# Fused encoder layer with product-key experts: the look-ahead shrinks from 96 to 72 expert blocks, and VectorE's and GpSimd's work around it is laid out anew

## What is computed

```
q  = rms_norm(h @ w_query)                    # 8 heads x 256
s1, s2 = scores of each half against 128 keys # top 16 of each
top_score, expert_idx = top 16 of the 256 sums # an index below 16384, per head
gate = softmax(top_score)
act  = gelu(u[expert_idx] . h) * gate          # 128 experts per token
x    = x + sum(act * v[expert_idx])
```

## Time and profile before

| | us |
|---|---|
| median of 3 runs (lowest, highest) | 3359.02 (3358.28, 3362.66) |
| the profiled execution: its own time | 3356.09 |
| its span, first to last instruction | 3354.4 |
| mean granted TensorE clock | 0.948 |
| TensorE busy | 2977.8 (89%) |
| VectorE busy | 2421.1 (72%) |
| GpSimd busy | 1695.2 (51%) |
| ScalarE busy | 1167.4 (35%) |
| DMA moved | 923.63 MB, 275 GB/s over the span |

### The profile page before, as it was taken

How to read it: one execution, slowest core, us unless ns; L and a number is a source line. 1 busy time by engine, 2 the same in 40 slices (tenths; PEclk the granted TensorE clock), 3 DMA queues, 4 the chain that set the end, 5 groups by cost and what they waited for, 6 DMA issues and landing times.

```text
span 3354.4 us, 43376 instructions
## 1 busy us (share of the span) xinstructions
PE 2977.8 (89%) x17829; PEld 2793.4 (83%) x17829; DVE 2421.1 (72%) x3297; ACT 1167.4 (35%) x1317; POOL 1695.2 (51%) x665
## 2 busy tenths in 40 slices
PE   6899899865989999987777998988888888999998
PEld 5677787644869999987777998888888888999998
DVE  5656566542676599997787345898888888767776
ACT  6756433344333333332222233222222222333332
POOL 0000443311232378864333687677677767667763
PEclk9999999977999999999888998999999999999999
DMA  7747458822696766656766998888888888888886
GB/s 299 266 163 286 156 215 311 311 75 86 261 359 259 264 242 235 235 181 206 244 213 212 339 381 335 329 339 328 327 335 327 317 336 335 325 345 335 345 326 233
DMA packets 196478, 923.63 MB, mean 275 GB/s; under 512 B 17712, under 2 KB 83360, under 8 KB 93376
## 3 DMA queue, kind: packets, MB, share of 16 engines
q1 hardware_dynamic: 85136, 479.24, 38.6%
q0 software_dynamic: 56112, 406.05, 32.0%
q10 hardware_dynamic: 55104, 36.71, 3.5%
HBM read 876.25 MB, written 45.61 MB: 275 GB/s over the span
## 4 chain that ended last, share of the span: by engine, by line
PE 47%; DVE 25%; DMA 15%; ACT 6%; issue 5%; ACTq 1%; POOL 1%; SPq 0%; DVEq 0%; POOLq 0%
PE ps L1473 6%; DMA rows<-peer_u_rows,idx_far 5%; PE ps L1782 5%; PE ps L1784 5%; PE ps L1783 5%; PE ps L1713 5%; PE ps L1714 5%; PE ps L1715 5%; DVE rows L1199 5%; PE ps L1698 3%; PE ps L1460 3%; DMA g_in<-gelu_scratch 3%; DVE g_in L1357 3%; DVE hot_b L1341 2%; DVE ring_lo L986 2%
## 5 line engine op out<-in xcount | busy, mean ns | idle before, releaser
L530 POOL TENSOR_TENSOR ring_lo<-ring_raw,ring_hi 128x2048 fp32r<-128x2048 f32 x252 | 1191.6, 4729 | 1047.0 <-ACT ring_hi L603 1045.8
L603 ACT ACTIVATE ring_hi<-ring_raw 128x2048 fp32r<-128x2048 f32 x400 | 763.6, 1916 | 696.8 <-DMA ring_raw<-w_in 204.6
L1782 PE MATMUL ps<-a_hi,ring_hi 128*128 128x320 f32 x2048 | 651.6, 318 | 102.9 <-DVE yT L1379 88.5
L1713 PE MATMUL ps<-bT_hi,ring_hi 128*128 128x320 f32 x2048 | 650.2, 317 | 10.1 <-ACT ahead L903 5.3
L1783 PE MATMUL ps<-a_lo,ring_hi 128*128 128x320 f32 x2048 | 643.8, 314 | 0.0
L1784 PE MATMUL ps<-a_hi,ring_lo 128*128 128x320 f32 x2048 | 643.4, 314 | 0.0
L1714 PE MATMUL ps<-bT_lo,ring_hi 128*128 128x320 f32 x2048 | 642.4, 314 | 0.0
L1715 PE MATMUL ps<-bT_hi,ring_lo 128*128 128x320 f32 x2048 | 641.8, 313 | 0.0
L986 DVE TENSOR_TENSOR ring_lo<-ring_raw,ring_hi 128x2048 fp32r<-128x2048 f32 x148 | 378.1, 2567 | 167.6 <-ACT ring_hi L603 167.3
L1782 PEld LDWEIGHTS ps<-a_hi,ring_hi 128*128 128x128 f32 x2048 | 394.6, 193 | 119.1 <-DVE yT L1379 96.6
L556 POOL DMA_INDIRECT rows<-peer_u_rows,idx_far x128 | 222.8, 1740 | 509.5 <-DVE z_far L1199 482.8
(11 more groups left out here) (285 smaller groups left out, 4171.7 us busy)
## 6 DMA issues: line engine op xcount, KB each, us to landing
ring_raw<-peer_u SPq DMA_DIRECT2D x128, 1024.0 KB, 5.3
ring_raw<-peer_v SPq DMA_DIRECT2D x128, 1024.0 KB, 7.3
ring_raw<-w_in SPq DMA_DIRECT2D x80, 1024.0 KB, 4.9
ring_raw<-w_out SPq DMA_DIRECT2D x32, 1024.0 KB, 5.0
ring_raw<-w_query SPq DMA_DIRECT2D x32, 1024.0 KB, 4.9
gates_scratch<-gbuf ACTq DMA_DIRECT2D x20, 1024.0 KB, 12.5
g_pair<-gates_scratch SPq DMA_DIRECT2D x64, 320.0 KB, 8.1
gelu_scratch<-ahead ACTq DMA_DIRECT2D x96, 160.0 KB, 5.5
```

The costliest lines, as they stand in the source:

```text
L530: pool.tensor_tensor(ring_lo[s][:], ring_raw[s][:], ring_hi[s][:].bitcast(F32), ALU.subtract)\
L603: act.activation(ring_hi[place(n)][:], ring_raw[place(n)][:], ACT.Copy).then_inc(hi_ok[SLOT[n]], 1)
L1713: pe.matmul(dst, hi[:, e], bT_hi[:, k, 0:NEAR], start=(k == 0), stop=False)
L1782: pe.matmul(dst, hi[:, col], a_hi[:, par, e, :], start=(e == 0), stop=False)
```

## The change

- `PRE` goes from 96 to 72: 24 blocks fewer in ahead and in down, 24 more in both (56 pairs). The downs are 68, the plain ups after the gate batches 5 instead of 29.
- In down (and for the first four blocks, during the last two ups) ScalarE copies `g_in` into a PSUM bank that is free (`gelu_to_psum`), and the gate product and the low half are made from PSUM. The product moves ahead of the row, the low half behind it.
- In the gate batches the low halves of four pieces in six, and of the last ahead pieces, go to VectorE; the other two stay on GpSimd. The one-hot ring gets a third place, `hot_b` is one instruction for four tokens, VectorE builds up to three sets ahead. The batch is 4, 4, 4, 4, 0, 0 outer products per up instead of 3, 3, 3, 3, 3, 1. The rows there go 1, 0, 1, 0, 2, 2.
- GpSimd issues a gather when the buffer's last row is 2 pieces behind, from the down stage on.
- The rows are spread anew: 60 instead of 47 at pieces 92 to 111 (20 instead of 12 of them in the attention), 28 and 30 instead of 28 and 28 at the two projections, 30 in the gate batches as before, 8 after them (38), 75 in down (123), 140 in both (77).
- In the attention ScalarE takes the two heads of a pair together through Abs, Exp and Ln; VectorE takes two rows ahead of the softplus and three behind the mask; the squares of y are summed in two parts.

```diff
-PRE = 96
+PRE = 72
 def lo_on_pool(n):
-    if n in POOL_A or AHEAD <= n < BOTH:
+    if n in POOL_A or DOWN <= n < BOTH or AHEAD <= n < AHEAD + HOT_FIRST:
         return True
+    if AHEAD <= n < DOWN:
+        return (n - AHEAD - HOT_FIRST) % len(HOT_BATCH) < 2
...
-ATTEND_ROWS = 12
+ATTEND_ROWS = 20
+HOT_RING = 3
+HOT_BATCH = (4, 4, 4, 4, 0, 0)
+HOT_ROWS = (1, 0, 1, 0, 2, 2)
...
+def gather_lag(n):
+    return 2 if n >= DOWN else ROW_LAG
...
-                gather_freed_before(n + 1 - ROW_LAG)
+                gather_freed_before(n + 1 - gather_lag(n))
...
             def load_gelu(i):
                 sp_eng.wait_ge(ahead_stored[i % 2], 16 * (i // 2 + 1))
                 if i >= 2:
-                    sp_eng.wait_ge(alo_made, i - 1)
+                    sp_eng.wait_ge(in_psum, i - 1)
...
+            def gelu_to_psum(i, bank):
+                act.wait_ge(gin_loaded[i % 2], 16 * (i // 2 + 1))
+                act.activation(ps[:, bank, 0:NEAR], g_in[i % 2][:], ACT.Copy).then_inc(in_psum, 1)
...
             for i in range(GROUP, PRE):
-                n = DOWN + i - GROUP
+                v = i - GROUP
+                n = DOWN + v
+                act.wait_ge(y_added, 4 * v + 1)
+                act.wait_ge(alo_made, GROUP)
+                gelu_to_psum(i, i % 4)
                 hi_upto(n + 2)
...
+            def hot(jj):
+                if jj >= HOT_RING:
+                    dve.wait_ge(g_mm, jj - HOT_RING + 1)
+                first, tok = 4 * (jj % HOT_RING), 4 * jj
+                for q in range(4):
+                    dve.tensor_scalar(hot_a[:, first + q, :], iota[:], selT[:, 0, tok + q:tok + q + 1],
+                                      selT[:, 2, tok + q:tok + q + 1], ALU.is_equal, ALU.mult)
+                dve.tensor_tensor(hot_b[:, first:first + 4, :], bcast(iota[:], [P, 4, NK], 1),
+                                  bcast(selT[:, 1, tok:tok + 4], [P, 4, NK], 2), ALU.is_equal).then_inc(hot_made, 1)
...
                 if v:
                     add_y(v - 1, 3)
-                rows_step(1 if ROWS_AT[n] else 0)
-                add_y(v, 0)
-                gate_down(i)
-                add_y(v, 1)
-                rows_step(ROWS_AT[n] - (1 if ROWS_AT[n] else 0))
+                dve.wait_ge(in_psum, i + 1)
+                gate(i, src, i // 4 + 1)
+                rows_step(1)
+                gated_lo(i, src)
+                add_y(v, 0)
+                add_y(v, 1)
+                rows_step(ROWS_AT[n] - 1)
                 add_y(v, 2)
...
-                    if k % 5 == 4 and k // 5 < gates_at:
+                    if k % 4 == 3 and k // 4 < gates_at:
                         outers()
...
-                    down(c, g + (USE0[c] + PRE // 4 + 1), 16 * g + 4 * c, c, par)
+                    down(c, g + (USE0[c] + PRE // 4 + 1), 16 * g + 4 * c, c, par, own=4 * g + (c + GROUP + 1))
```

More of the change, by code:

```diff
@@ L109, in fill_rows @@
             ROWS_AT[AHEAD + AHEAD_TILE * t + 2 + 2 * r] = 1
-    for i in range(HOT_FIRST, PRE):
-        ROWS_AT[AHEAD + i] = 1 if i < HOT_FIRST + 30 or i % 3 else 2
+    for i in range(HOT_FIRST, HOT_END):
+        ROWS_AT[AHEAD + i] = HOT_ROWS[(i - HOT_FIRST) % len(HOT_ROWS)]
+    for i in range(HOT_END, PRE):
+        ROWS_AT[AHEAD + i] = 2 if i < PRE - 2 else 1
     for n in range(DOWN, BOTH):
-        ROWS_AT[n] = 2 if n % 3 == 0 else 1
-    left = N_ROWS - sum(ROWS_AT)
-    spots = list(range(BOTH, LAST))
+        ROWS_AT[n] = 2 if n % 10 == 0 else 1
+    left, spots = N_ROWS - sum(ROWS_AT), range(BOTH, LAST)
     for j, n in enumerate(spots):
@@ L956, in _ @@
                 if i % GROUP == 0 and i > GROUP:
-                    act.wait_ge(freed[SLOT[n - 1]], USE[n - 1])
-                a_hi_of(i, g_in[i % 2][:])
+                    wait_piece(act, n - 1)
+                a_hi_of(i, ps[:, i % 4, 0:NEAR])
             for m in range(NK - PRE):
@@ L1253, in _ @@
                     norm_qk(i + 1)
+                rows_step(2)
                 for ab in range(2):
@@ L1361, in gate, with gate_first, hots_upto @@
                    .then_inc(alo_made, 1)
-            def gate_down(i):
-                dve.wait_ge(gin_loaded[i % 2], 16 * (i // 2 + 1))
-                gate(i, g_in[i % 2][:], i // 4 + 1)
+            def gate_first(i):
+                src = ps[:, i % 2, 0:NEAR]
+                dve.wait_ge(in_psum, i + 1)
[10 more added lines that the diff above has]
+                                  bcast(selT[:, 1, tok:tok + 4], [P, 4, NK], 2), ALU.is_equal).then_inc(hot_made, 1)
+            jj = [0]
+            def hots_upto(count):
+                while jj[0] < min(count, N_HOT):
+                    hot(jj[0])
+                    jj[0] += 1
+            hots_upto(HOT_RING)
+            used = 0
+            for i in range(HOT_FIRST, PRE):
+                lo_upto(min(AHEAD + i + 2, DOWN - 1))
+                used += HOT_AT[i]
+                hots_upto(used + HOT_RING)
+                if i < PRE - 2:
+                    rows_step(ROWS_AT[AHEAD + i])
+                else:
+                    gate_first(2 * (i - PRE + 2))
+                    rows_step(ROWS_AT[AHEAD + i])
+                    gate_first(2 * (i - PRE + 2) + 1)
+            assert jj[0] == N_HOT
             def v_piece(v):
@@ L1379, in add_y @@
                     dve.tensor_tensor(dst, src, dst, ALU.add).then_inc(y_added, 1)
-            for i in range(GROUP):
-                gate_down(i)
             for i in range(GROUP, PRE):
```

92 lines of the change are left out of this document (52 added, 40 removed).

## The result

The changed kernel takes **3227.89 us** (median of 4 runs, 3213.22 to 3231.14) against 3360.84 (3358.28 to 3370.47, 4 runs) of the kernel before beside it: ratio 0.9592, 95% interval 0.9562 to 0.9623, so 133 us faster by the medians. The forecast was 3152 with a range of 3095 to 3225: the sign and most of the mechanisms were right, the size too large. The median lies 3 us above the range; the ratio, put on the 3359.02 from which the forecast started, gives 3222, just inside it.

What follows compares the result with a forecast made beforehand. VectorE, stretched by GpSimd's low halves, slowed down, the largest term. Down -294, both +334, plain ups -177, change to down -4.5, batches -59, input +21, attention -27 gave -206.5 from 3356.09; with 2.9 for the median, 3152 us (3095 to 3225).

Steps and rivals of the forecast that it cites:

- Down, -294: Down: with product and low half made from PSUM, 68 pieces at 7.25 us, 493 us against 787.
- the chain of `g_in`: Down: from load issue to halved gate, 2T = L + 5.35 us; load time L = 8.7 gives 7.04 a piece.
- The sign that I had named for this being wrong: Down: VectorE's gate product waiting for `g_in` in most pieces would show the forecast wrong.
- the first rival: Down: the load of `g_in` sets the pace at 8.0 us or more, +51, 3203 us; chance 0.17.
- Only operations with both inputs in SBUF are stretched.: VectorE in down: the product from SBUF takes 1585 ns in the mean, from PSUM 496, beside a busy GpSimd.
- Both, +334: Both: 24 more pairs at 13.84 us, +332, and 2 us added.
- Ups, batches, change to down, -240.5: 24 fewer plain ups -177, change to down -4.5, gate batches at 68 us each -59.
- Before the expert layer, -6: Input stage +21 for its added rows; attention -27 from its new order of work.
- Transfers did not bound both: Rival: transfers bound both at 7.38 us a piece, and down too; +50 and +9, 3211 us; chance 0.11.
- the stores did hold the sixth up: Rival, gate batches: stores don't hold up the sixth up, batches of 58 us, -50 more, 3102 us; chance 0.12.
- the product from PSUM was not stretched: Rival: the product from PSUM is stretched all the same, down stays at 8.55 us, +88, 3240 us; chance 0.03.
- gathers sooner did no harm: Rival, down and both: gathers issued sooner delay GpSimd's low halves, making the kernel slower, 3368 us; chance 0.03.

Runs made afterwards that it cites:

- experiment 1: The changed kernel with gate product and low half reading the loaded gelu in SBUF again from the fifth block of down on; 3341.68 us, ratio 0.9942.
- experiment 2: The changed kernel with the loads of gates and gelu of down issued ahead of the piece load instead of behind it; 3202.23 us, ratio 0.9517.
- experiment 7: The changed kernel with all low halves of the gate batches on GpSimd again; 3249.93 us, ratio 0.9692.
- g1_combined: The changed kernel with earlier gelu loads, split stores, earlier row counts in input stage and attention, first gates ahead of the last ups' rows; 3135.40 us, ratio 0.9348.
- Experiment 9: The run of g1_combined: five edits put together on the changed kernel, among them both first gates ahead of the rows in the last two ups; 3135.40 us.
- Experiments 4: The changed kernel with the row counts ahead of the expert layer as in the kernel before; 3196.74 us, ratio 0.9495.
- experiment 10: g1_combined with 30 instead of 35 rows in the input stage and 8 instead of 12 in attention; 3125.75 us, ratio 0.9286.
- e5_pre96: The changed kernel with the split at 96 blocks again (PRE = 96), all the rest as changed; 3259.60 us, ratio 0.9696.
- e2_stores_split: The changed kernel with a batch's four gate stores split, two behind the fourth up's gelu and two behind the fifth's; 3199.73 us, ratio 0.9511.

## Why the prediction was right in sign and too large

**Down, -294 against -275.7.** The main step held: operations with one input in PSUM at 0.50 us, the clock at 0.99, VectorE no longer the bound (experiment 1). The term was mis-sized by the chain of `g_in`. I put L = 8.7 us and said that 10 would give 7.7 a piece; the stage came out at 7.53, although the loads landed in 4.7 / 7.5 / 10.6 us (shortest, median, longest), so that by my formula the median would have done no harm. Which link of that chain I had too short is open. The sign that I had named for this being wrong did show: VectorE's gate product waited for the copy of `g_in` in 44 of 68 pieces, 68.9 us in all. It was the first rival in kind, though not in size (+18 instead of +51), and experiment 2 shows it by taking the wait away.

One statement of the prediction is too narrow, without harm to the sum: "Only operations with both inputs in SBUF are stretched." `hot_a` takes one tile from SBUF, and it averaged 532 ns before where one undisturbed takes 340; experiment 7 shows it again.

**Both, +334 against +336.1.** Right to 2 us, but by luck, since two errors cancel. The price of a pair was 0.3 us too low (7 us for 24): 443 us divided by 32 pairs gave 13.84, while the window held 31.3 pairs, and from gelu to gelu a pair takes 14.14 before. And where I added 2 us for the denser traffic, a pair became 0.06 us shorter, 14.08 (774.5 over 55), 3 us in all. The transfers do not bound it: TensorE is busy for all of it, at a share of 0.90. At 0.93 (g1_combined) 13 rows more cost 10 us.

**Ups, batches, change to down, -240.5 against -233.8.** The batches came out as forecast. From one batch's stores to the next's pass 67.6 to 68.2 us, where I said 68: 24.3 from the stores to the gelu of the sixth up (24 said), with the gelu of the fourth held for 14.5 (16.8 said) and TensorE idle for 8.8, and 43.3 for the next four ups. From the first outer product to the end of the fifth batch's sixth up the stage takes 338.3 us (1484.7 to 1822.98) and took 398 (1454.0 to 1852): -59.7 against -59. A set costs VectorE 2.06 us instead of the 1.65 that I put, which does no harm: TensorE waits 0.3 us for one-hots, and GpSimd, with two low halves in six, hardly held `hot_a` (its longest was 473 ns). The plain ups and the change to down did worse, -174.1 against -181.5. I counted back 4.5 us for gates laid beside the last two ups, and did not see that the first of them stands behind VectorE's rows, whose gathers land late in this traffic; TensorE waits 8.7 us for the first low half, where it stood still for 7 before. Experiment 9 shows that moving two products ahead of one up's rows is not enough. On the chain of after:

```profile
1830.02 11.13 DMA rows<-peer_v_rows,idx_far
...
1843.81 13.09 DMA rows<-peer_v_rows,idx_far
```

**Before the expert layer, -6 against +30.7.** This is the step that failed, with 37 of the 64 us by which the profiled executions miss the forecast. It failed in the room that I gave the rows: in the input stage I let one of the five new rows go free, and in the attention I put what stands around the rows at 9.0 us. For the input stage I priced four rows at 5.14. Five rows at 5.39 are 27 us, and the other 35 cost 0.25 more each, 9: together 36 against the 34.1 by which the stage grew, more than the end of +26 that I gave it. For the attention I had the new order of work right in kind (worth 35.1), and the rows between mask and softplus came near what I said (20.4 us, from 778.08 to 798.47, against 22.1). What I put at 4.0 + 4.4 + 0.6 = 9.0 us around them is 13.5: the chain runs serially through VectorE's softplus products (1.9), TensorE's 10.98 for both heads (the row of 800.45 above) and the masks (0.6). The pair takes 33.9 instead of 31.1, and the last pair has no room at all: its three rows stand ahead of the norm. So the stage gave 9.8 us and not 27 (in the other kernels with the same order 3 to 7). Experiments 4 and 9 confirm the cause: without the extra rows these two stages give 52 to 62 us back. The query and retrieval stages cost 6.4 us more, which I put at nothing. One execution cannot show a cause for that: the queries alone took 167.6 us before, 172.6 after, and 169.7 to 188.8 in the eight other kernels with the same lists.

**The rivals.** Transfers did not bound both; the stores did hold the sixth up; the product from PSUM was not stretched; gathers sooner did no harm. The median lies 76 us above the forecast. The upper end of the range was built from the rivals for down and both, while the largest miss lay ahead of the expert layer, for which no rival was named.

**Open.** The changed kernel's four runs are 3213 once and 3228 to 3231 three times, and only the first was profiled. In the profiles of the kernels with the same lists the queries vary most (by 19 us), which may be where the 15 us lie; why they vary is not known. The division of the batches' gain beyond the third buffer and the low halves stays unexplained.

## What to carry to other kernels

An operation's price on a shared engine is set by where its operands lie and by what the other engine does in that moment: look for groups whose mean is far above their median, and move one operand to PSUM before moving work. Work that is spread "into the gaps" should be priced at each place by the chain it joins: the same row cost 0.8 to 1.1 us in both, 3.2 in attention and 5 to 7 in the input stage, as long as it stood on the path; four fewer in the attention, once it did not, gave nothing (experiment 10). And a small load on which a chain rests should be issued before its engine stops to wait for the free slot of a big one.

## What of the hardware was not expected

- A gather of 1 MiB stood on the chain for 5.6 to 7.4 us in the attention (share 0.40 from 702 to 865; the last for 12.3), for 7.1 to 11.2 in the input stage (0.79), and for 11.7 to 17.6 us at a share of 0.98 (e5_pre96).
- The wide one-hot with two SBUF inputs was never held beside GpSimd's low halves (672 to 687 ns in 79 operations of e7_low_on_gpsimd), while `hot_a`, with one input tile in SBUF, was held for up to 5.35 us. Each wide one follows four `hot_a`, which may take the hit for it; this was not separated.
- Four stores of the gates hold ScalarE for 14.1 to 14.6 us, two for 3.9 to 9.6 us (e2_stores_split); where they stand in its list decides what they cost.
